# Second attention: low parts of 14 weight chunks on GpSimd, convolution steps and layer norm moved forward

## What is computed

```python
proj = u @ w_in
q, k, v, c_in, g = jnp.split(proj, [...], axis=-1)
y_a = chunked_attention(q, k, v, rel_table) @ w_attn_out      # 8 heads of 64
y_b = conv_module(c_in, ...)                                   # below
gates = jax.nn.sigmoid(g + gate_bias)
merged = gates[..., :D_MODEL] * y_a + gates[..., D_MODEL:] * y_b
return merged @ w_out

def conv_module(...):        # 512 channels
    c = (c_in + bias)[..., :512] * sigmoid(c_in[..., 512:])
    c = depthwise convolution over time, 31 taps, + dw_b
    c = jax.nn.silu(layer_norm(c, ln_g, ln_b))
    return c @ w_out
```

## Time and profile before

| | |
|---|---|
| median of 3 runs | 1978.5 us (1968.16 to 2380.15) |
| the profiled execution | 1979.01 us, span 1977.4 us |
| PE busy | 1878.4 us, 95% |
| DVE, ACT, POOL busy | 53%, 37%, 2% |
| granted TensorE clock, mean | 0.974 |

### The profile page before, as it was taken

One profiled execution on the slowest core, in us unless ns is written; L12 is line 12 of the kernel. 1 busy time (PEld: TensorE's weight loads), 2 busy tenths in 40 slices (PEclk: granted clock), 3 DMA queues, 4 the chain that ended last, 5 costly groups with the idle time before them and its releaser, 6 DMA issues.

```text
span 1977.4 us, 22785 instructions
## 1 busy us (share of the span) xinstructions
PE 1878.4 (95%) x8816; PEld 1547.8 (78%) x8816; DVE 1038.2 (53%) x1478; ACT 738.5 (37%) x1008; POOL 49.3 (2%) x100
## 2 busy tenths in 40 slices
PE   4999999989999999999999999998888999999998
PEld 4788888867878888778888888886566788888887
DVE  5436666458456666654444225598755463333313
ACT  3445554233345545432322114223343252222212
POOL 1000000000000000100000000000000000000000
PEclk7999999989999999999999999998989999999999
DMA  8346555422212221233342323241212223333231
GB/s 322 130 135 184 173 175 173 134 68 86 79 50 64 64 64 43 86 85 95 96 116 76 128 86 86 86 128 43 64 43 85 86 64 106 103 99 95 99 104 64
DMA packets 246680, 201.12 MB, mean 102 GB/s; under 512 B 6386, under 2 KB 225860, under 8 KB 245572
## 3 DMA queue, kind: packets, MB, share of 16 engines
q1 hardware_dynamic: 238048, 166.25, 28.5%
q0 software_dynamic: 8064, 33.56, 4.8%
q10 hardware_dynamic: 484, 0.16, 0.0%
HBM read 197.83 MB, written 2.11 MB: 101 GB/s over the span
## 4 chain that ended last, share of the span: by engine, by line
PE 87%; DVE 7%; issue 2%; ACT 2%; DMA 1%; DVEq 0%; POOL 0%; ACTq 0%; POOLq 0%
PE acc L654 12%; PE acc L656 12%; PE acc L655 12%; PE sc L1022 5%; PE acc L1022 3%; PE acc L844 3%; PE acc L846 3%; PE acc L845 3%; PE tr L1022 2%; PE ob L1022 2%; PE misc L1022 2%; PE acc L1209 1%; PE acc L1210 1%; PE acc L1211 1%; DMA s_ada_w<-in_a_ada_w 1%
## 5 line engine op out<-in xcount | busy, mean ns | idle before, releaser
L1793 DVE TENSOR_TENSOR s_w_low<-s_raw,s_w_high 128x2048 fp32r<-128x2048 f32 (+1 forms) x149 | 337.1, 2263 | 374.7 <-ACT s_w_high L1287 374.6
L1287 ACT ACTIVATE s_w_high<-s_raw 128x2048 fp32r<-128x2048 f32 x151 | 284.6, 1885 | 204.2 <-PE acc L1022 174.6
L654 PE MATMUL acc<-s_h_high,s_w_high 128*128 128x512 f32 x880 | 345.1, 392 | 1.6 <-DVE s_sg L2358 1.6
L656 PE MATMUL acc<-s_h_high,s_w_low 128*128 128x512 f32 x880 | 342.6, 389 | 0.0
L655 PE MATMUL acc<-s_h_low,s_w_high 128*128 128x512 f32 x880 | 342.5, 389 | 0.0
L654 PEld LDWEIGHTS acc<-s_h_high,s_w_high 128*128 128x128 f32 x880 | 165.3, 188 | 35.8 <-issue 2.4
L656 PEld LDWEIGHTS acc<-s_h_high,s_w_low 128*128 128x128 f32 x880 | 165.2, 188 | 34.2
L655 PEld LDWEIGHTS acc<-s_h_low,s_w_high 128*128 128x128 f32 x880 | 165.3, 188 | 33.8 <-issue 0.2
L844 PE MATMUL acc<-s_h_high,s_w_high 128*128 128x512 f32 x256 | 108.7, 425 | 2.2 <-DVE s_w_low L1793 1.4
L1665 ACT ACTIVATE s_hid_high<-s_hd 128x512 fp32r<-128x512 f32 x44 | 27.8, 632 | 219.0 <-DVE s_hd L2367 118.6
L846 PE MATMUL acc<-s_h_high,s_w_low 128*128 128x512 f32 x256 | 102.9, 402 | 0.0
(11 more groups left out here) (438 smaller groups left out, 3436.9 us busy)
## 6 DMA issues: line engine op xcount, KB each, us to landing
s_raw<-in_a_w_in SPq DMA_DIRECT2D x48, 512.0 KB, 5.0
s_raw<-in_ffn_w_gate SPq DMA_DIRECT2D x44, 512.0 KB, 3.9
s_raw<-in_ffn_w_up SPq DMA_DIRECT2D x44, 512.0 KB, 5.1
s_raw<-in_ffn_w_down SPq DMA_DIRECT2D x40, 512.0 KB, 4.3
s_raw<-in_w_in SPq DMA_DIRECT2D x36, 512.0 KB, 4.2
s_raw<-in_b_w_in SPq DMA_DIRECT2D x32, 512.0 KB, 4.8
s_ada_w<-in_b_ada_w POOLq DMA_DIRECT2D x24, 512.0 KB, 5.3
s_ada_w<-in_a_ada_w POOLq DMA_DIRECT2D x8, 1024.0 KB, 12.4
```

Source lines behind the costliest of these rows:

```text
L654: pe.matmul(bank[b][:, :], w_high[:, o:o + P], hi, start=(k == 0), stop=False, skip_group_check=grouped)
L656: mm = pe.matmul(bank[b][:, :], w_low[:, o:o + P], hi, start=False, stop=(k == nk - 1), skip_group_check=grouped)
L1287: act.activation(w_high[:, part], raw[:, part], ACT.Copy).then_inc(w_high_ready, 1)
L1793: dve.tensor_tensor(w_low[:, w], raw[:, w], w_high[:, w].bitcast(F32), ALU.subtract).then_inc(w_ready, 1)
```

## The change

1. `POOL_LOWS` names the chunks mix + 5 to mix + 9, gates 0 to 7 and outs 0: 14 chunks. GpSimd makes their low parts with the same `tensor_tensor`, each behind ACT's high part; DVE no longer does, and waits once, ahead of "outs", until all are made.
2. Beside each of the mixer's last six chunks DVE makes 4 x 4 = 16 convolution steps and not 12: 4 + 96 = 100 of 124 are done ahead of the attention (76 before). The remaining 24 go at 2 a row, on rows 0 to 11 (48 at 3 a row on rows 0 to 15 before).
3. `LN_AT` is 13 and not 16: all of the layer norm comes three rows earlier, on PE, ACT and DVE.

```diff
--- before.py
+++ after.py
@@ -67,6 +67,7 @@
 ROWS = {"dn1": DN, "wo": WO, "dn2": DN}
 USED0 = {"dn1": 0, "wo": len(DN) - 1, "dn2": len(DN) + len(WO) - 2}
 TOK0 = {"dn1": 0, "wo": TT, "dn2": 2 * TT}
+POOL_LOWS = C0["mix"] + 5, C0["outs"] + 1
 HALF_CHUNKS = {C0[name] + c for name in ("dn1", "dn2") for c in range(2)}
 
 
@@ -125,7 +126,7 @@
 
 
 WARM = 12
-LN_AT = 16
+LN_AT = 13
 SILU_AT, SILU_LOW_AT = (9, 10, 12, 14), (11, 13, 14, 15)
 ROW_COUNTS = (sum(n for _, n in ROWS_A), sum(n for _, n in ROWS_B), CONV * CT)
 
@@ -638,6 +639,12 @@
                 w = slice(s * SLOT, (s + 1) * SLOT)
                 pool.tensor_tensor(w_low[:, w], raw[:, w], w_high[:, w].bitcast(F32), ALU.subtract).then_inc(w_ready, 1)
 
+            pool.wait_ge(w_ready, POOL_LOWS[0])
+            for c in range(*POOL_LOWS):
+                pool.wait_ge(w_high_ready, c + 1)
+                w = slice(c % 2 * SLOT, (c % 2 + 1) * SLOT)
+                pool.tensor_tensor(w_low[:, w], raw[:, w], w_high[:, w].bitcast(F32), ALU.subtract).then_inc(w_ready, 1)
+
         @block.tensor
         def _(pe):
             def product(b, tq, s, where, t, high, low, k0, nk, ready=None, base=0, between=None, bank=acc):
@@ -2399,9 +2406,8 @@
             for n in range(CT):
                 dve.tensor_scalar(cy[:, n * T:(n + 1) * T], glu[:, n * GW:n * GW + T], col("conv_dw_w_2", n),
                                   col("conv_dw_b_2", n), ALU.mult, ALU.add).then_inc(conv_step, 1)
-            taps = 3
+            taps = 4
             for m in range(6):
-                next_low(q0 + 2 + m // 2, m % 2)
                 with dve.Fori(0, taps) as i:
                     for n in range(CT):
                         dve.wait_ge(conv_step, i * CT + (m * taps * CT + n + 1))
@@ -2491,24 +2497,22 @@
                                              in1=conv_out[n][:, :].bitcast(F32), op0=ALU.mult, op1=ALU.subtract)\
                        .then_inc(conv_ready, 1)
 
-            q0 = C0["gates"] // 2
             for n in range(H2 * TT):
                 softmax2(n)
                 if n > 0:
                     scale2(n - 1)
                 if n > 8 and n % 8 == 2:
                     output2(n // 8 - 1)
-                for e in range(CT * (6 * taps + 1) + 3 * n, min(CT * (6 * taps + 1) + 3 * n + 3, CT * CONV)):
+                for e in range(CT * (6 * taps + 1) + 2 * n, min(CT * (6 * taps + 1) + 2 * n + 2, CT * CONV)):
                     dve.wait_ge(conv_step, e - CT + 1)
                     tap(e // CT, e % CT)
-                if n % 4 == 0:
-                    next_low(q0 + n // 8, n // 4 % 2)
                 conv_norm(n - LN_AT)
             scale2(H2 * TT - 1)
             output2(H2 // 2 - 1)
 
 
             q0, t0 = C0["outs"] // 2, T0["outs"]
+            dve.wait_ge(w_ready, POOL_LOWS[1])
             for b in range(2):
                 dve.wait_ge(evac[b], T0["outs"] // 2)
             with dve.Fori(0, 2) as i:
```

## The result

The changed kernel takes 1999.17 us (median of 4 runs, 1997.11 to 2003.63), the kernel before 1974.12 beside it. The ratio is 1.0128, with a 95% interval of 1.0100 to 1.0157: slower by 1.3%, inside the forecast's range of times but not the "no change" that was forecast. Two executions were disturbed, one of 2380.15 us of the kernel before and one of 4091.97 us in experiment 6: the ratios leave them out, while the medians 1974.12 here and 1963.01 there still count them. The profiled executions are 2000.06 us and 1979.01 us, a difference of 21.05 us to be found in the traces.

The account below looks back on a forecast made before the run. PE, busy 95% of the span, was taken as the bound, with idle time and lost clock in the second attention. 1979.0 + 27.0 (mixer) - 31 (attention) + 0 (norm) gave 1975 us, no measurable change; range 1955 to 2010.

Parts of the forecast that it names:

- part 2: Beside the mixer's chunks: GpSimd gets in behind a running step and blocks DVE, so the attention begins 27.0 us later.
- rival B: Mixer: DVE's overlapping steps do not let GpSimd in until all 96 end; attention 57 us late, 2005 us; chance 0.13.
- The forecast's 27.0 us: Mixer: six GpSimd low parts each block DVE's steps for 4.5 us, and nothing hides it.
- B's turning point: Mixer: being kept out decides once GpSimd waits longer than PE's spare 3.7 us, six steps.
- Rival A: GpSimd's low parts do not exclude convolution steps; mixer's loss 0, attention's gain 37 us, 1942 us; chance 0.12.
- 138 us: Second attention's length after the change, 127.8 + 7 + 3, in place of 169.35: a gain of 31.
- the slow first 6 us: Start of the second attention: the first 6 us run at the low clock as now, costing 3 us.
- The 127.8 us of work at full clock: Second attention without waits at full clock: 169.35 x 0.89 - 22.9 us.
- The four new waits of 1.7 us: Second attention, rows n = 4, 12, 20, 28: `scale2` locked out by GpSimd makes PE wait, 7 us in all.
- Rival C: Attention: clock falls after each new wait, or waits are not covered: 7 + 12 us more, 1987 to 1994; chance 0.15.
- The norm's move: Layer norm three rows earlier in the attention: costed at nothing, or 0.6 us without cover.
- The test named ahead: Profile after, mixer: steps keeping 0.74 us mean no exclusion; GpSimd instructions lasting tens of us mean it is kept out.

Follow-up runs that it names:

- experiment 6: Kernel before, only the low parts of gates 1 to outs 0 moved to GpSimd, three steps a row and the norm's row kept: 1963.01 us, ratio 0.9915.
- Experiment 1: Changed kernel with the mixer's 96 convolution steps issued from an unrolled loop, no hardware loop: 2000.02 us.
- 4: Changed kernel with the second input of the mixer's 96 steps read from PSUM, leaving out the running sum: 1956.67 us.
- 2: Changed kernel with DVE waiting for GpSimd's low part ahead of each of the six groups of 16 steps: 1976.74 us.
- 3: Changed kernel with one small single-input DVE instruction, a one-column reciprocal, ahead of each group of 16 steps, no wait added: 1976.58 us.
- experiment 5: Changed kernel with DVE waiting for its own last steps to drain ahead of each group of 16 steps: 1978.31 us.
- 10: Changed kernel with DVE waiting for its own last convolution step before every four steps, 24 short pauses: 1983.01 us.
- 12: Changed kernel, 8 steps a group, five a row in the attention, norm at 16, each group waiting for a PE mark ahead of GpSimd's start: 1977.11 us.
- experiment 9: Kernel before with the changed kernel's attention; mixer low parts stay on DVE, 24 left-over steps run where DVE stood idle: 1943.5 us, ratio 0.9836.
- experiment 7: Changed kernel with GpSimd's low parts beside the mixer alone, the attention's back on DVE, two steps a row, norm from row 13: 2028.52 us.
- experiment 11: Changed kernel, 8 steps a group, five a row in the attention, norm at 16, each group waiting for ACT's high part: 1983.99 us.

## Why the prediction was wrong

**The step that failed** is the sentence of part 2 that lets GpSimd's low part in after "up to 0.7 us of a running step". Instead rival B came: DVE's steps kept it out for the whole block. B was worked out at 57 us of lateness and 2005 us; 55.5 us and 1999.17 were measured. That B came so close is partly luck: it had the low part of mix + 5 kept out and PE stopping at about 1280. In the trace that one got in at 1269.35 beside the starting steps, the next was kept out, and PE stopped at 1288.43. The forecast's 27.0 us were 28.5 too few; the attention's 1.7 us more of gain and the start 1.7 us earlier take off 3.4, which leaves the 25 us between 1975 and the profiled 2000.06. Experiment 1 excludes the loop, 4 shows that the second SBUF input is needed for it, and 2, 3 and 5 show that a break at each sixteenth step brings the forecast back (1976.6 to 1978.3 us, with 26.9 to 28.1 us for the mixer's part).

**B's turning point** was put too finely. "Six steps" was where PE's spare time ends, if GpSimd is kept out from any point on. The runs show a second condition: it matters when GpSimd asks. The runs show it let in when it asks within the first four steps of a block (1395.87, experiments 3, 10, 12; that of 1269.35 asked in the third starting step, a `tensor_scalar`), and kept out when it asks in the eighth (experiment 5), the ninth (1280.07, experiments 2, 3, 12) or later. In the attention DVE has two steps between other instructions, so it never matters. Why DVE's run passes over GpSimd only once it is some steps old is open, and so is the point between the fourth and the eighth step, and whether steps or time count (2.2 us into a block against 5.2); no run here looks into it.

**Right: exclusion and its price.** Six low parts were put at 27.0 us. The traces show 28.0, 26.9 and 28.1 (experiments 2, 3 and 5). Rival A, no exclusion, falls by `scale2`'s 2.06 us and the 5.75 us of two steps.

**The attention: the mechanism right, its 138 us in part by luck.** 138 us were forecast. Where PE comes to it from a wait for the copies, as the forecast had it, it takes 137.96 to 138.91 us (experiments 2, 3, 5 and 10), and 138.26 in experiment 9. In the changed kernel it is 136.75, since the slow first 6 us fell on the chunks before it: PE is busy 131.42 us in it, against 133.94 in experiment 9. So 2.5 us moved out of this stage; they are part of the 55.5. But the terms of the 138 were off both ways. The 127.8 us of work at full clock came from the mean clock over the whole window, its idle time too; at a granted clock of 1.00 the same 635 matmuls are 131.42 us, 3.6 more. Against that, PE's idle time was put at 7 us and is 4.3 in experiment 9 (133.94 busy of 138.26).

**Sizes that were off.** The four new waits of 1.7 us (7 us) are seven of at most 1.0 and 4.2 in sum. Rival C, slow clock behind new waits, falls: the clock is 1.00. Waits of 2 us, for which C was named, did not come, so what the clock does behind those isn't shown. The norm's move was put at nothing and is worth 2.5 us. The first of the six low parts falls on the starting steps (6.21 us for 1.91), not on the others; the sum of six isn't changed by it.

**The test named ahead** held: "if GpSimd's instructions last tens of us, B". One did, with 62.33 us.

## What to carry to other kernels

Before work goes from VectorE to GpSimd, look at what VectorE runs beside it: if those are instructions with two SBUF inputs, nearly each microsecond on GpSimd is taken from VectorE (six low parts of 4.6 us cost it 27 to 28), and if many of them follow each other without a gap, GpSimd may not start until they end. A single-input instruction or a drain of 0.3 us at the points where GpSimd should get in restores it; better still is to leave such a stretch alone, as experiment 9 does, and offload where VectorE's instructions read PSUM, or where such instructions come in ones and twos and VectorE has time to spare. Two terms of 30 us that cancel are a reason to build them apart: each alone showed its sign at once (1963 and 2029 us).

## What the runs showed of the hardware that was not expected

- A GpSimd instruction (`tensor_tensor` of 128x2048 f32 within SBUF) was kept out for 58 us (1280.07 to 1338.04) by a run of VectorE instructions with two SBUF inputs each, 0.66 us apart, while VectorE lost nothing. It was let in behind the running instruction when it asked within four of such a run's start, and not when it asked in the eighth or later.
- A VectorE instruction of 0.15 us with one input, or an idle time of about 0.3 us, ends this at once.
- With the second input in PSUM both engines keep their pace: 4.63 us and 0.66 us a step.
- A wait of VectorE on its own last instruction costs 0.36 us: four steps take 3.01 us with it and 2.65 without, of which the record shows 0.27 as idle time.
- After 54 us without work TensorE's granted clock is 0.56 over the next 6.6 us: the low level for nearly all of them.
- The point where the mixer's starting steps begin varies between 1266.3 (experiment 7) and 1275.5 us (experiment 11) among kernels whose code is the same up to there. Stages, not totals, should be compared for differences of a few us.
